# Both halves of an attention block's first projection chunk on unnormed activations, and a forget gate's split weights in one stationary tile

## The reference, cut to what matters

```python
h = rms_norm(x, ln1_g) * (1 + sc1) + sh1          # 512 x 1024
u = h @ w_in
fq, fk, fv, fg, dq, dk, dv = split(u)             # fg: 8 columns
fq, fk = rms(heads(fq), g[0]), rms(heads(fk), g[1])   # over 64 columns of a head
log_f = log_sigmoid(fg + b_f)                     # log(sigmoid(t)) = min(t, 0) - log(1 + exp(-|t|))
cum = cumsum(log_f, axis=tokens)                  # added to the logits of the first attention
```

## Time and profile before

| | |
|---|---|
| median of 3 runs | 1366.52 us (1365.45 to 1366.68) |
| profiled execution, first to last instruction (span) | 1364.9 us |
| median less span | 1.6 us |
| PE busy | 1357.1 us, 99% |
| DVE busy | 1058.3 us, 78% |
| ScalarE busy | 718.1 us, 53% |
| granted TensorE clock, mean | 1.000 |

### The profile page before, as it was taken

One profiled execution on the slowest core, in us unless ns is written; L12 is line 12 of the kernel. 1 busy time (PEld: TensorE's weight loads), 2 busy tenths in 40 slices (PEclk: granted clock), 3 DMA queues, 4 the chain that ended last, 5 costly groups with the idle time before them and its releaser, 6 DMA issues.

```text
span 1364.9 us, 21409 instructions
## 1 busy us (share of the span) xinstructions
PE 1357.1 (99%) x7911; PEld 1164.9 (85%) x7911; DVE 1058.3 (78%) x1787; ACT 718.1 (53%) x1261; POOL 50.9 (4%) x55
## 2 busy tenths in 40 slices
PE   8999999999999999999999999999999999999999
PEld 6998888888889878888888787787687998998997
DVE  6976777777799788888888868878867965983883
ACT  5744233333357566656664567766746642662561
POOL 0001000000100000000001100000030000000000
PEclk9999999999999999999999999999999999999999
DMA  9995444557743211111211231211122232333232
GB/s 377 392 371 196 169 169 181 184 212 269 291 160 109 93 62 63 62 63 65 83 68 62 93 124 63 65 60 63 60 96 72 84 132 77 104 122 124 75 114 90
DMA packets 35350, 181.51 MB, mean 133 GB/s; under 512 B 4153, under 2 KB 4921, under 8 KB 20930
## 3 DMA queue, kind: packets, MB, share of 16 engines
q1 hardware_dynamic: 34050, 177.95, 35.9%
q10 hardware_dynamic: 1216, 2.44, 0.6%
HBM read 177.74 MB, written 2.11 MB: 132 GB/s over the span
## 4 chain that ended last, share of the span: by engine, by line
PE 98%; DVE 1%; ACT 0%; issue 0%; DMA 0%; DVEq 0%; ACTq 0%
PE acc L2147 74%; PE turn L2770 7%; PE ada L2147 4%; PE turn L2147 3%; PE norm L2147 3%; PE ada L2770 2%; PE acc L2770 2%; PE norm L2770 2%; PE turn L2613 1%; PE turn L2459 1%; DVE w_lo L1227 0%; DVE s L1816 0%; ACT w_hi L682 0%; DVE q_n L1219 0%; DMA c_in<-in_c 0%
## 5 line engine op out<-in xcount | busy, mean ns | idle before, releaser
L2147 PE MATMUL acc<-h_hi,w_hi 128*128 128x512 f32 x696 | 277.8, 399 | 0.0
L2147 PE MATMUL acc<-h_hi,w_lo 128*128 128x512 f32 x696 | 272.0, 391 | 0.0
L2147 PE MATMUL acc<-h_lo,w_hi 128*128 128x512 f32 x696 | 271.3, 390 | 0.0
L1227 DVE TENSOR_TENSOR w_lo<-w_raw,w_hi 128x2048 fp32r<-128x2048 f32 x58 | 136.5, 2353 | 30.6 <-ACT w_hi L682 30.6
L2147 PEld LDWEIGHTS acc<-h_hi,w_lo 128*128 128x128 f32 x696 | 130.6, 188 | 28.3
L2147 PEld LDWEIGHTS acc<-h_hi,w_hi 128*128 128x128 f32 x696 | 130.8, 188 | 26.8 <-issue 0.4
L2147 PEld LDWEIGHTS acc<-h_lo,w_hi 128*128 128x128 f32 x696 | 131.0, 188 | 25.5
L682 ACT ACTIVATE w_hi<-w_raw 128x2048 fp32r<-128x2048 f32 x60 | 114.4, 1907 | 29.3 <-PE acc L2147 28.5
L1219 DVE SCALAR_TENSOR_TENSOR x<-acc,mods,x 128x512 f32<-128x512 f32 x48 | 38.7, 814 | 68.6 <-PE acc L2147 68.4
L2147 PE MATMUL acc<-wv_hi,h_hi 128*128 128x256 f32 x320 | 89.6, 281 | 0.0
L2147 PE MATMUL acc<-wv_lo,h_hi 128*128 128x256 f32 x320 | 88.3, 277 | 0.0
(11 more groups left out here) (380 smaller groups left out, 3480.5 us busy)
## 6 DMA issues: line engine op xcount, KB each, us to landing
w_raw<-in_weights SPq DMA_DIRECT2D x102, 1024.0 KB, 4.9
ada_v<-in_ada SPq DMA_DIRECT2D x32, 512.0 KB, 6.3
ada_raw<-in_ada SPq DMA_DIRECT2D x32, 512.0 KB, 5.8
ada_out<-in_ada SPq DMA_DIRECT2D x32, 512.0 KB, 6.5
ada_up<-in_ada_first SPq DMA_DIRECT2D x8, 1024.0 KB, 16.8
w_raw<-in_weights SPq DMA_DIRECT2D x4, 768.0 KB, 4.3
x<-in_x SPq DMA_DIRECT2D x2, 1024.0 KB, 5.9
w_first<-in_weights SPq DMA_DIRECT2D x4, 512.0 KB, 13.4
```

The lines of the kernel that those rows point to most:

```text
L1227: nc.vector.tensor_tensor(lo[:, 0:used], w_raw[par][:, 0:used], f32(hi[:, 0:used]), ALU.subtract).then_inc(lo_done, 1)
L2147: return nc.tensor.matmul(out, lhsT, rhs, start=start, stop=stop)
```

## The change

The border takes the form of the feed-forward one. `raw_chunk` runs both halves unnormed (48 matmuls of 512 columns where there were 24), with the shift sums as two rows. In the normed part PE has the gates alone, and these by two matmuls a tile: the gates' hi and lo weights lie in columns 0 to 7 and 32 to 39 of one stationary tile `wf_two`, which meets h_hi and h_lo (16 matmuls where the gates and the key half had 48). The low product comes out in rows 32 to 39 and DVE adds it; the product lo with lo, left out before, is now in the sum. DVE also makes the absolute value. The first two head tiles now take the raw way (rescale, shift, gain). ACT rounds chunk W_Q2 + 2 right behind the normed tiles, and DVE splits it behind head tile 0. The squares of head tiles 0 and 1 are summed after step kt = 3 and kt = 4 of the next chunk's halves (kt = 1 before), those of tile 3 after block (5, 0) of the values (in its middle before).

The uses of the renamed tiles, the new semaphore and the callers at the other border are left out.

```diff
--- before.py
+++ after.py
...
@@ -290,12 +290,13 @@
     pt_2 = [at(f"pt_2{s}", [P, TOK], up + 64 * KB + 2 * KB * s) for s in range(3)]
     lam_rows = at("lam_rows", [P, 256], T[8])
     lam_prod = at("lam_prod", [P, 128], T[8] + KB)
-    wf_hi = at("wf_hi", [P, KT, P], up + 56 * KB, F32R)
-    wf_lo = at("wf_lo", [P, KT, P], up + 60 * KB, F32R)
+    wf_two = at("wf_two", [P, KT, P], up + 56 * KB, F32R)
+    gate_part = at("gate_part", [8, TOK], T[5])
+    gate_full = at("gate_full", [8, TOK], T[7])
     gate_abs = at("gate_abs", [8, TOK], T[5])
     gate_exp = at("gate_exp", [8, TOK], T[5])
     gate_ln = at("gate_ln", [8, TOK], T[5])
-    gate_min = at("gate_min", [8, TOK], T[7])
+    gate_min = at("gate_min", [8, TOK], T[8])
     gate_log = at("gate_log", [8, TOK], T[7])
     gate_one = at("gate_one", [8, TOK], off_ada + 6 * KB)
     cum = at("cum", [8, TOK], T[8])
...
@@ -706,9 +707,9 @@
                     nc.scalar.activation(four(dst) if dilate else dst, dilated(src) if dilate else src, ACT.Identity,
                                          bias=mods[:, shift + kt:shift + kt + 1]).then_inc(hhi_done, 1)
 
-            def shift_row(n):
-
-                act.wait_ge(bias_done, 3)
+            def shift_row(i, n):
+
+                act.wait_ge(bias_done, i + 1)
                 nc.scalar.activation(sh_row[:, 0:n * P], AD[0:2, 0:n * P], ACT.Copy).then_inc(sh_row_out, 1)
 
             def x_round(i, m, dilate=False):
...
@@ -955,10 +956,13 @@
                         nc.scalar.activation(weights_at(u, par)[0][:, 1024:2048], w_raw[par][:, 1024:2048], ACT.Copy).then_inc(hi_done, 1)
                     x_round(1, m)
             rstd_start(N_X2, NB[:, :], DM, True)
-            h_round(3, SHIFT_1, False, range(KT))
+            h_round(3, SHIFT_1, False, range(4))
+            shift_row(1, 2)
+            h_round(3, SHIFT_1, False, range(4, KT))
+            to_hi(*divmod(W_Q2 + 2, 2))
             act.wait_ge(bias_ready, 2)
             act.wait_ge(acc_freed, 2 * W_Q2 - 15)
-            square(pre[2], sq_hi_2, sq[0], w_shift[:, 0:1])
+            square(pre[0], sq_hi_2, sq[0], w_shift[:, 0:1])
 
             def head_square(mi, bank):
                 k = norm2(0, mi)
...
@@ -966,15 +970,13 @@
                 act.wait_ge(sum_done, k)
                 square(bank, sq_hi_2, sq[0])
 
-            act.wait_ge(fg_done, 1)
-            nc.scalar.activation(gate_abs[:, :], T0[0:8, :], ACT.Abs, bias=bf_col[:, :]).then_inc(fgate_act, 1)
+            rstd_start(norm2(0, 0), NB[:, :], 64, True)
+            act.wait_ge(acc_freed, 2 * W_Q2 - 14)
+            square(pre[1], sq_hi_2, sq[0], w_shift[:, 1:2])
+            act.wait_ge(fgate_dve, 4)
+            nc.scalar.activation(gate_exp[:, :], gate_abs[:, :], ACT.Exp, scale=-1.0).then_inc(fgate_act, 1)
+            act.preload_act_table_set("natural_log")
             act.wait_ge(fgate_act, 1)
-            nc.scalar.activation(gate_exp[:, :], gate_abs[:, :], ACT.Exp, scale=-1.0).then_inc(fgate_act, 1)
-            to_hi(*divmod(W_Q2 + 2, 2))
-            rstd_start(norm2(0, 0), NB[:, :], 64, True)
-            head_square(1, G[1])
-            act.preload_act_table_set("natural_log")
-            act.wait_ge(fgate_act, 2)
             nc.scalar.activation(gate_ln[:, :], gate_exp[:, :], ACT.Ln, bias=ones[0:8, 0:1]).then_inc(fgate_act, 1)
             act.preload_act_table_set("natural_log_exp_and_others")
 
...
@@ -1008,7 +1010,7 @@
                     act.dma_start(c_rows[kind][:, :, :], rows.partition_broadcast(P)).then_inc(c_row_loaded, 16)
 
             rstd_start(norm2(0, 1), NB[:, :], 64)
-            act.wait_ge(fgate_dve, 4)
+            act.wait_ge(fgate_dve, 6)
             act.dma_start(cum_dram, cum[:, :]).then_inc(cum_stored, 16)
             head_square(2, G[2])
             spread_load()
...
@@ -1358,8 +1360,8 @@
 
             def shift_sum(i, n):
 
-                if i == 2:
-                    dve.wait_ge(sh_turned, 1)
+                if i > 0:
+                    dve.wait_ge(sh_turned, i)
                     nc.vector.tensor_copy(w_shift[:, 0:n], AD[:, 2 * P:2 * P + n]).then_inc(bias_ready, 1)
                 else:
                     dve.wait_ge(bias_done, i + 1)
...
@@ -1771,25 +1773,34 @@
             x_rest(1, KT - 1)
             x_norm(N_X2, 3, 1)
             h_split(3, SHIFT_1, False)
-            shift_sum(1, 1)
-            rescale(2, G[0][:, :], 2 * W_Q2 + 1)
-            square_rest(31, sq_hi_2, sq[0], sq_lo_2)
-
-
-            dve.wait_ge(fgate_act, 1)
-            nc.vector.tensor_scalar(gate_min[:, :], T0[0:8, :], bf_col[:, :], 0.0, ALU.add, ALU.min).then_inc(fgate_dve, 1)
+            shift_sum(1, 2)
+            for half in range(2):
+                rescale(half, G[half][:, :], 2 * W_Q2 + half + 1)
             dve.wait_ge(bias_ready, 2)
-            dve.wait_ge(acc_freed, 2 * W_Q2 - 15)
-            shifted(qk[0][0][:, :], pre[2][:, :], w_shift[:, 0:1], gains[:, 1:2], 3)
-            to_lo(*divmod(W_Q2 + 2, 2))
+            for half in range(2):
+                dve.wait_ge(acc_freed, 2 * W_Q2 - 15 + half)
+                shifted(qk[0][half][:, :], pre[half][:, :], w_shift[:, half:half + 1], gains[:, 1 + half:2 + half], 3 + half)
+                if half == 0:
+                    square_rest(31, sq_hi_2, sq[0], sq_lo_2)
+
+
+            dve.wait_ge(fg_done, 1)
+            nc.vector.tensor_copy(gate_part[:, :], T0[32:40, :]).then_inc(gate_joined, 1)
+            dve.wait_ge(gate_joined, 1)
+            stt(gate_full[:, :], T0[0:8, :], bf_col[:, :], gate_part[:, :], ALU.add, ALU.add).then_inc(fgate_dve, 1)
+            dve.wait_ge(fgate_dve, 2)
+            nc.vector.tensor_scalar(gate_min[:, :], gate_full[:, :], 0.0, None, ALU.min).then_inc(fgate_dve, 1)
+            dve.wait_ge(fgate_dve, 3)
+            stt(gate_abs[:, :], gate_min[:, :], -2.0, gate_full[:, :], ALU.mult, ALU.add).then_inc(fgate_dve, 1)
             scale_first(norm2(0, 0), qk[0][0][:, :], qk[0][0][:, :], 1.0)
             newton(norm2(0, 0), 64)
+            scale_last(norm2(0, 0), qk[0][0][:, :])
             square_rest(32, sq_hi_2, sq[0], sq_lo_2)
-            scale_last(norm2(0, 0), qk[0][0][:, :])
-            dve.wait_ge(fgate_act, 3)
-            dve.wait_ge(fgate_dve, 2)
+            to_lo(*divmod(W_Q2 + 2, 2))
+            dve.wait_ge(fgate_act, 2)
+            dve.wait_ge(fgate_dve, 4)
             nc.vector.tensor_tensor(gate_log[:, :], gate_ln[:, :], gate_min[:, :], ALU.subtract).then_inc(fgate_dve, 1)
-            dve.wait_ge(fgate_dve, 3)
+            dve.wait_ge(fgate_dve, 5)
             nc.vector.tensor_tensor_scan(cum[:, :], gate_one[:, :], gate_log[:, :], 0.0, ALU.mult, ALU.add).then_inc(fgate_dve, 1)
 
 
...
@@ -1871,8 +1882,11 @@
                     dve.wait_ge(inv2_done, i0 + 3)
                     stt(p1, s_2[n % 3][:, 1, 0:width], lam_inv[:, 0:1], p1, ALU.mult, ALU.add).then_inc(p2_ready, 1)
 
-            def head_normed(mi, bank):
-                scale_first(norm2(0, mi), qk[0][mi][:, :], bank[:, :], gains[:, 1 + mi:2 + mi]).then_inc(acc_freed, 1)
+            def head_normed(mi, bank=None):
+                if bank is None:
+                    scale_first(norm2(0, mi), qk[0][mi][:, :], qk[0][mi][:, :], 1.0)
+                else:
+                    scale_first(norm2(0, mi), qk[0][mi][:, :], bank[:, :], gains[:, 1 + mi:2 + mi]).then_inc(acc_freed, 1)
                 newton(norm2(0, mi), 64)
                 if mi == 2:
                     rest2(norm2(0, 3))
...
@@ -1883,7 +1897,7 @@
                 nc.vector.tensor_copy(v_2[t % 2][:, 2 * half:2 * half + 2, :], G[half][:, :].rearrange("p (t n) -> p t n", t=2))\
                     .then_inc(acc_freed, 1)
 
-            head_normed(1, G[1])
+            head_normed(1)
             rest2(norm2(0, 2))
             to_lo(*divmod(W_Q2 + 3, 2))
             head_normed(2, G[2])
...
@@ -2213,9 +2227,9 @@
                 if kts[-1] == KT - 1:
                     last.then_inc(bias_done, 1)
 
-            def shift_turn(halves):
-
-                pe.wait_ge(sh_row_out, 1)
+            def shift_turn(n, halves):
+
+                pe.wait_ge(sh_row_out, n)
                 for half in range(halves):
                     last = mm(AD[:, 2 * P + half:2 * P + half + 1], sh_row[:, P * half:P * half + P], ones[0:2, 0:1], True, True)
                 last.then_inc(sh_turned, 1)
...
@@ -2565,19 +2579,19 @@
 
             pe.wait_ge(s_freed, 4 * QH)
             output(W_OUTB, yb_hi, yb_lo_of, yblo_done, (7,), (0, 4))
-            raw_chunk(1, W_Q2, 1, xg_hi, xg_lo_of, 2 * W_Q2 - 17, 2, N_X2)
+            raw_chunk(1, W_Q2, 2, xg_hi, xg_lo_of, 2 * W_Q2 - 17, 2, N_X2)
             def head_squares(k, lhs):
                 sum_squares(k, k - N_2 + 31, lhs, sq_hi_2, sq_lo_2)
 
             pe.wait_ge(wflo_done, 1)
             pe.wait_ge(half_ready, 2)
-            pe.wait_ge(acc_freed, 2 * W_Q2 - 16)
             for kt in range(KT):
                 h_ready(3, kt)
```

(32 more changed lines are left out.)

## The result

The kernel after the change takes 1371.53 us (median of 5 runs, 1370.89 to 1373.91), the kernel before 1366.52 (1365.45 to 1368.79).

A forecast was written before the change was run, and what follows sets the result against it. PE was taken to bound the kernel, DVE the normed stretch. Terms: -0.1 at the gates, +0.4 or 0.5 until tile 3's squares, +0.95 at the scores, together +1.3 us, giving 1367.8 us; range 1366.0 to 1369.8.

The forecast's parts named there:

- PE is through at 764.39 + 14.66: Unnormed chunk on PE: starts at 764.39 as before, lasts 14.66 us, ends at 779.05 instead of about 773.4.
- The norm, h_lo and the gates: Normed part: sum 2.99 us after the chunk, h_lo 1.39 later, last ends 784.39, next chunk 785.0 against 785.07.
- eight saved matmuls become holes: Gates on PE: matmuls worth 1.8 us saved bring 0.1 us and become 1.5 us of holes.
- Squares of tile 0, the join, DVE's queue: Behind the gates: no PE wait for squares, 0.3 us spare; four gate steps 2.7 us; scan ends 797.2, 2.2 later.
- I take 0.3, nearer nothing, for the store is small: Running sum's store, now meeting a weight load: 0.3 us added, bounded between 0 and some 2 us.
- the rival with this size: Store in traffic: ScalarE's queue waits for it, each microsecond reaches PE; at +2, 1369.5 us; chance 0.10.
- Its upper bound, the weight load's own busy time: Store in traffic: most the weight load could add to it, some 2 us.
- The scores' wait: First scores on PE: new wait of about 1.0 us (0.95 in the sum), fewer matmuls covering tile 3's norm.
- Nothing behind, and no fall of the clock: After the first scores no further waits, broadcast loads in time; holes cost nothing; clock rival 1372.3 us, chance 0.04.

The follow-up runs named there:

- a1: Changed kernel, with the unnormed chunk waiting only until its own two banks are free, not for the last updates of x; ratio to the kernel before 1.0022.
- a4: Kernel before with the gates alone changed: one stationary weight tile, two matmuls a step instead of three, low product not added; ratio to the kernel before 1.0.
- b3: b2 with the norm's sum of squares behind 9 matmuls of the unnormed chunk instead of 12; ratio to the kernel before 1.0002, run again 1.0.
- a2: Changed kernel, with SP's weight load for chunk W_Q2 + 4 held until the running sum's store has landed; ratio to the kernel before 1.0027.
- d1: b3 with head tile 2's 24 matmuls put among the gate matmuls, squares of head tiles 0 and 1 moved; ratio to the kernel before 1.0026.
- c1: Kernel before, with SP's weight load for chunk W_Q2 + 4 delayed so that it flows during the running sum's store; ratio to the kernel before 1.0013.
- a3: Changed kernel, with ScalarE rounding the fourth chunk ahead of the wait for the store and the broadcast loads; ratio to the kernel before 1.0022.
- b1: Changed kernel with the edits of a1 and a3 together; ratio to the kernel before 1.0007.
- b2: b1 with head tile 3's squares summed in the middle of the value block again; ratio to the kernel before 1.001.

## Why the prediction was wrong

Sorted by its steps; the scores came 2.78 us later than forecast (813.43 against 810.65).

1. **"PE is through at 764.39 + 14.66": the length was right, the start was not.** From first matmul to the end of the unnormed part are 14.76 us (14.66 forecast). But the step took the start of before over unchanged and never asked what a second half waits for. The wait for the other half's count moved to the front: 1.44 us in the bracket, 1.60 from start to start, 1.77 in the border of a1 (there the brackets behind are 0.17 shorter too). No term and no rival of the prediction had it. The prediction had asked what a moved step waits for with DMAs and roundings, and not with PE's own semaphores.
2. **The norm, h_lo and the gates: right.** The sum started 3.07 us after the chunk (2.99 forecast); the last h_lo ended at 784.19 + 1.62 = 785.81, 1.42 over the forecast, which is item 1; the next chunk at 786.44 against 785.0, again item 1. That eight saved matmuls become holes held here and in a4.
3. **Squares of tile 0, the join, DVE's queue: right.** No wait before the squares. The four gate steps took 0.68, 0.74, 0.42 and 0.68, 2.5 for the 2.7 taken. The scan ended at 798.54, forecast 797.2 and item 1's 1.4.
4. **"I take 0.3, nearer nothing, for the store is small": the mis-sized term.** It measured 3.25 - 1.49 = 1.76 above the quiet round trip, so 1.46 more than taken. The mechanism, its place in ScalarE's queue and the rows behind were named; the rival with this size had a chance of 0.10 and was what happened. The store's size was the wrong thing to go by: of the 1.76 us, 1.51 lie ahead of its first packet, which waits while the load's packets go. Its upper bound, the weight load's own busy time, was the right thing. The Trainium skill (DMA: Bandwidth & Descriptors, Latency and other measured facts) puts an access to HBM at 0.2 us on average and at 2 us under high load, and says that this makes most of a DMA's fixed cost. By these two figures the term would be up to 1.8 us, an estimate; the size agrees with the runs (1.4 to 1.8 above the quiet 1.49, last section), the place does not, as the traces have most of it ahead of the store's first packet and not behind its last.
5. **The scores' wait: right**, 0.93 against 0.95. The squares of tile 3 to the scores took 4.38 (4.33 forecast).
6. **Nothing behind, and no fall of the clock: right.** DVE made its masks at 814.40 without a wait for the broadcast loads. Holes of 1.44, 1.75 and 0.93 us stand at a granted clock of 1.00. By the rule on micro-idling in the Trainium skill (TensorE: Matmul & The Clock Gate, A second HAM failure mode: psum-queue depth-cycling) the clock might have swung between its levels; no trace here shows it.

The sum: 1.3 forecast, 1.60 for the start and 1.46 for the store give 4.36; the border grew by 4.32. Either term alone would have left the time in the stated range (1367.8 + 1.6 = 1369.4, under 1369.8); it took both. The runs settle both terms: they go one by one (1.77; 1.67 or 1.77) and together (3.69), which leaves 0.6. That is about what an earlier norm sum gives back (0.76 in b3). The medians differ by 5.0, 0.7 more than the border; the profiled execution of after, 1370.89, is the fastest of its five and 0.6 under their median.

## What to carry to other kernels

When a step is moved or widened, list the semaphore counts that its first instruction asks for, also on the engine that bounds the kernel, and read in the trace when each is reached; the wait that cost 1.60 us here had cost nothing before only because of where it stood. A small store whose completion holds an in-order queue is priced by what is left of the load ahead of it, so a wait for it goes behind everything that others need, or the big load goes behind the store. And work taken from PE in a stretch that another engine paces is worth next to nothing (0.16 of 1.8 us in a4), while work put there delays whatever hangs on the stretch's last result.

## What was not expected of the hardware

**A store's round trip under a load.** From the issue of 16 KB to the issue of the loads that wait for it: 1.49 (before), 1.50 (a4) and 1.51 us (a2) with the queues quiet, against 2.85 (d1), 2.97 (c1) and 3.18 to 3.29 us (after, a1, a3, b1, b2, b3 twice) where the 1 MB load goes out ahead of it. Nothing lies between. By the packets of ScalarE's queue, the store's first one starts 0.79 or 0.80 us after the issue in the three quiet traces and 1.90 to 2.48 in the nine others; each 2 KB packet takes 0.08 us under the load. In the nine, the load's first packet lies 0.80 us (after) to 1.23 us (d1) ahead of the store's issue, and from it to the issue of the waiting loads are 3.97 to 4.17 us in every one. So the round trip ends with the load, and is the shorter the later the store is issued. Why the load's packets go first is open.

**Two levels ahead of the border.** The profiles of b1, b2 and b3 (twice) start the chunk at 766.07 to 767.33, the others at 763.2 to 764.4 once the wait is taken off. The groups of PE up to 763 show where. First the kernel before, then b3 again:

```profile
L2147 PE MATMUL acc<-wv_hi,h_hi 128*128 128x256 f32 x192 | 53.0, 278 | 0.0
L2147 PE MATMUL acc<-wv_lo,h_hi 128*128 128x256 f32 x192 | 52.7, 276 | 0.0
L2147 PE MATMUL acc<-wv_hi,h_lo 128*128 128x256 f32 x192 | 51.9, 276 | 0.0
```

```profile
L2161 PE MATMUL acc<-wv_hi,h_hi 128*128 128x256 f32 x192 | 53.9, 282 | 0.0
L2161 PE MATMUL acc<-wv_lo,h_hi 128*128 128x256 f32 x192 | 53.6, 281 | 0.0
L2161 PE MATMUL acc<-wv_hi,h_lo 128*128 128x256 f32 x192 | 52.8, 281 | 0.0
```

The same 576 matmuls of the first attention's values, in code that no edit touches, take 2.7 us more in all four late profiles and in none of the eight others, at a granted clock of 1.00 in each. That is the distance of the two groups of times. Why it happens, and why in these four, is open. The profiles of b2 and of the first b3 have another 0.8 us behind the feed-forward border, which the second b3 doesn't have.
